# Start of the projections: small loads on ScalarE's queue, free signals first, first rows scaled at once, query weights a head per round

## The reference

```python
h = rms_norm(x, g_mix)
q, k, v, f_logit, a, gate = split(h @ w_in)        # 3 x 512, 8, 2 x 512 columns
logf = log_sigmoid(f_logit + b_f)                  # per row and head
attn = softmax(q k^T / 8 + cumsum(logf) terms, causal) v
u = a * sigmoid(gate)
conv = silu(layer_norm(depthwise_conv31(u) + b_dw))
x = x + concat(attn, conv) @ w_out
x = x + peer_ffn(rms_norm(x, g_ffn))               # 8 heads, 16 of 16384 experts each, rows gathered
y = rms_norm(x, g_final)
```

## Time and profile before

| | us |
|---|---|
| median of 3 runs | 3392.09 |
| lowest and highest | 3391.64, 3394.30 |
| the profiled execution | 3393.65 |
| its span, first to last instruction | 3391.9 |
| busy: TensorE 73%, DVE 72%, POOL 42%, ACT 30% of the span | |
| mean granted TensorE clock | 0.869 of full speed |
| gathers of expert rows (1088), share of the 16 DMA engines' span | 83.0% |
| query-weight loads | 8 of 1024 KB |
| store of turned keys, per round | 260 KB |

### The profile page before, as it was taken

One profiled execution on the slowest core, in us unless ns is written; L12 is line 12 of the kernel. 1 busy time (PEld: TensorE's weight loads), 2 busy tenths in 40 slices (PEclk: granted clock), 3 DMA queues, 4 the chain that ended last, 5 costly groups with the idle time before them and its releaser, 6 DMA issues. The chain is left out here.

```text
span 3391.9 us, 42114 instructions
## 1 busy us (share of the span) xinstructions
PE 2480.5 (73%) x13551; PEld 1076.9 (32%) x13551; DVE 2438.2 (72%) x6866; ACT 1021.4 (30%) x2925; POOL 1427.7 (42%) x1266
## 2 busy tenths in 40 slices
PE   5999867766866687767777776687767766776665
PEld 2444542322322233323323332333333322222221
DVE  2888757777777777777777776777677767677885
ACT  2333323223232323332333233323233233222321
POOL 0233344444444434443444444444444444444443
PEclk8999889888888888888888888888888888888887
DMA  7111429999999999999999999999999999999997
GB/s 253 56 56 47 134 110 412 416 415 403 415 407 410 399 411 403 408 406 410 400 405 399 410 404 401 404 405 401 408 400 412 405 411 409 388 392 420 419 414 313
DMA packets 220330, 1220.19 MB, mean 360 GB/s; under 512 B 34138, under 2 KB 61474, under 8 KB 80869
## 3 DMA queue, kind: packets, MB, share of 16 engines
q0 software_dynamic: 156672, 1140.92, 83.0%
q1 hardware_dynamic: 63461, 76.83, 6.8%
HBM read 1199.12 MB, written 18.55 MB: 359 GB/s over the span
## 5 line engine op out<-in xcount | busy, mean ns | idle before, releaser
L1269 POOL DMA_INDIRECT uv_rows<-in_uv_emb,experts x1088 | 1263.9, 1162 | 1607.1 <-PE ps L1373 1406.4
L1373 PE MATMUL ps<-uv_rows,diag 64*64 64x512 f32 x8704 | 1325.7, 734 | 823.8 <-ACT diag L1637 823.0
L1850 DVE CUSTOM_DVE_ANT_0 uv_rows<-uv_rows,handed 128x1024 f32<-128x1024 f32 x1088 | 1331.1, 1224 | 656.1 <-DMA uv_rows<-in_uv_emb,experts 651.0
L1373 PEld LDWEIGHTS ps<-uv_rows,diag 64*64 64x64 f32 x8704 | 321.7, 153 | 1477.1 <-ACT diag L1637 1059.4
L1629 ACT ACTIVATE gelu_c<-dots 128x2 f32<-128x2 f32 x544 | 110.7, 204 | 1649.6 <-DVE dots L1850 1648.6
L1637 ACT ACTIVATE diag<-ident_twice,act_c 128x64 f32<-128x64 f32 x1088 | 319.2, 340 | 283.9 <-DVE act_c L1867 282.9
L1333 PE MATMUL ps<-w_pq_sb,xnT_c 128*128 128x256 f32 x1152 | 342.7, 428 | 0.7 <-ACT xnT_c L1596 0.7
L1333 PEld LDWEIGHTS ps<-w_pq_sb,xnT_c 128*128 128x128 f32 x1152 | 219.9, 207 | 250.7 <-issue 227.4
L567 PE MATMUL ps<-w_in_sb,w_out_sb 128*128 128x512 f32 (+1 forms) x656 | 242.7, 525 | 17.5 <-ACT w_out_sb L453 17.5
L625 DVE SCALAR_TENSOR_TENSOR handed<-w_out_sb,tapsT,handed 128x128 f32<-128x128 f32 x960 | 252.8, 346 | 0.0
L388 POOL TENSOR_TENSOR rstd_a<-ms_a,neg_half 128x1 f32<-128x1 f32 x9 | 81.1, 9015 | 207.8 <-ACT ms_a L434 207.8
(11 more groups left out here) (247 smaller groups left out, 2166.8 us busy)
## 6 DMA issues: line engine op xcount, KB each, us to landing
uv_rows<-in_uv_emb,experts POOLq DMA_INDIRECT x1088, 13.2
w_in_sb<-in_w_in SPq DMA_DIRECT2D x4, 2048.0 KB, 12.0
w_pq_sb<-in_w_pq SPq DMA_DIRECT2D x8, 1024.0 KB, 12.3
w_out_sb<-in_x_prompt SPq DMA_DIRECT2D x8, 512.0 KB, 4.0
handed<-in_x_prompt SPq DMA_DIRECT2D x8, 512.0 KB, 3.4
w_out_sb<-in_w_out SPq DMA_DIRECT2D x1, 4096.0 KB, 19.2
out<-handed SPq DMA_DIRECT2D x8, 512.0 KB, 8.1
keys_turned<-handed SPq DMA_DIRECT2D x10, 260.0 KB
```

Of the source, the lines that this page charges most:

```text
L1269: nc.gpsimd.indirect_dma_start(out=rows[:, m % RING, :], out_offset=None, in_=d.uv_emb[0], in_offset=bass.IndirectOffsetOnAxis(ap=experts[ ...
L1373: ins = pe.matmul(ps[dst, 2 * x + half, :], diag[src, (m + i) % DIAGS, :], rows[src, (m + i) % RING, cols], start=first, stop=last)
L1850: nc.vector.tensor_tensor_reduce(out=row, in0=row, in1=xn[:, block_of(n) % 2, :], scale=1.0, scalar=0.0, op0=ALU.mult, op1=ALU.add, accum_ ...
```

## The change

The nine small loads are issued by ACT, ahead of its first mean square, with the cached log-forgets before the cached keys. SP's five increments stand right behind the load of block 0's rows, and all weights of w_in are issued without a break. `normed(0)` follows `row_scale(0)` directly, ahead of the copies of the setup. The query weights are loaded one head at a time: head b in `round_of(b)` right after the rows of the next block, the eighth after the sample rows.

```diff
--- before.py
+++ after.py
@@ -276,10 +276,8 @@
         @block.sync
         def _(sp):
             sp.dma_start(x[:, :], d.x_prompt[0, 0:P, :]).then_inc(x_here, 16)
-            sp.dma_start(vecs[0:s.DCH, :], d.g_mix[0].rearrange("(c p) -> c p", p=P)).then_inc(small_here, 16)
-            for i, v in enumerate((d.b_dw, d.ln_g, d.ln_b)):
-                lo = s.DCH + i * s.CCH
-                sp.dma_start(vecs[lo:lo + s.CCH, :], v[0].rearrange("(c p) -> c p", p=P)).then_inc(small_here, 16)
+            for stored, by in ((k_stored, 16), (kT_stored, 16), (q_stored, 16), (v_stored, 32), (conv_stored, 16)):
+                sp.sem_inc(stored, by)
             w_rows = d.w_in[0].rearrange("(c p) n -> p c n", p=P)
 
             def load_weights(name):
@@ -290,14 +288,12 @@
                     to = lo - s.DA if lo > COLS["v"][0] else lo
                     sp.dma_start(w_in[:, :, to:to + width], w_rows[:, :, lo:lo + width]).then_inc(w_here[name], 16)
 
-            load_weights(ORDER[0])
-            sp.dma_start(taps[:, :], d.w_dw[0]).then_inc(small_here, 16)
-            sp.dma_start(state[:, :], d.state_conv[0, 0]).then_inc(small_here, 16)
-            sp.dma_start(bf[:, :], d.b_f[0].partition_broadcast(P)).then_inc(small_here, 16)
-            sp.dma_start(k_aug[:, :, 0:s.HD], d.cache_k[0, 0]).then_inc(past_here, 16)
-            sp.dma_start(logf_past[:, :], d.cache_logf[0, 0]).then_inc(past_here, 16)
-            for name in ORDER[1:]:
+            for name in ORDER:
                 load_weights(name)
+
+            def load_query_weights(h):
+                hs = slice(h * 2 * s.HALF, (h + 1) * 2 * s.HALF)
+                sp.dma_start(g.w_pq[:, :, hs], d.w_pq[0][:, hs].rearrange("(c p) n -> p c n", p=P)).then_inc(g.w_pq_here, 16)
 
             def store_keysT(kb):
                 sp.dma_start(d.kT[:, :, bass.ds(kb * P, P)].rearrange("h e t -> e h t"), c.keysT).then_inc(kT_stored, 16)
@@ -324,21 +320,18 @@
             def round_of(b):
                 sp.wait_ge(xn_ready, b + 1)
                 sp.dma_start(x[:, :], d.x_prompt[0, bass.ds((b + 1) * P, P), :]).then_inc(x_here, 16)
+                load_query_weights(b)
                 if b > 0:
                     store_conv(b - 1)
                 stores(b, b, k_rows[bass.ds(b * P, P)], v_rows[bass.ds(b * P, P), :], P)
 
-            for stored, by in ((k_stored, 16), (kT_stored, 16), (q_stored, 16), (v_stored, 32), (conv_stored, 16)):
-                sp.sem_inc(stored, by)
             sp.wait_ge(kT_ready, PAST)
             store_keysT(s.NB)
-            for h in range(s.PH):
-                hs = slice(h * 2 * s.HALF, (h + 1) * 2 * s.HALF)
-                sp.dma_start(g.w_pq[:, :, hs], d.w_pq[0][:, hs].rearrange("(c p) n -> p c n", p=P)).then_inc(g.w_pq_here, 16)
             for b in range(s.NB - 1):
                 round_of(b)
             sp.wait_ge(xn_ready, s.NB)
             sp.dma_start(x[0:s.TS, :], d.x_sample[0]).then_inc(x_here, 16)
+            load_query_weights(s.PH - 1)
             store_conv(s.NB - 2)
 
             first = c.first
@@ -491,16 +484,25 @@
                 act.wait_ge(v_stored, 32 * b + 32)
                 each(b, nc.scalar.copy, c.values, ps[:, V_, :]).then_inc(v_ready, 1)
 
+            act.dma_start(vecs[0:s.DCH, :], d.g_mix[0].rearrange("(c p) -> c p", p=P)).then_inc(small_here, 16)
+            for i, v in enumerate((d.b_dw, d.ln_g, d.ln_b)):
+                lo = s.DCH + i * s.CCH
+                act.dma_start(vecs[lo:lo + s.CCH, :], v[0].rearrange("(c p) -> c p", p=P)).then_inc(small_here, 16)
+            act.dma_start(taps[:, :], d.w_dw[0]).then_inc(small_here, 16)
+            act.dma_start(state[:, :], d.state_conv[0, 0]).then_inc(small_here, 16)
+            act.dma_start(bf[:, :], d.b_f[0].partition_broadcast(P)).then_inc(small_here, 16)
+            act.dma_start(logf_past[:, :], d.cache_logf[0, 0]).then_inc(past_here, 16)
+            act.dma_start(k_aug[:, :, 0:s.HD], d.cache_k[0, 0]).then_inc(past_here, 16)
             for free in (q_ready, k_ready, v_ready):
                 act.sem_inc(free, 1)
             row_scale(0)
+            normed(0)
             act.wait_ge(setup_psum, 3)
             nc.scalar.copy(c.tapsT[:, :, :], ps[:, Q_, 0:s.CCH * s.TAPS].rearrange("p (c j) -> p c j", c=s.CCH)).then_inc(setup_sb, 1)
             nc.scalar.copy(g.vecT[:, :], ps[:, K_, 0:NVEC]).then_inc(setup_sb, 1)
             nc.scalar.copy(stateT[:, :, :], ps[:, V_, 0:s.CCH * HALO].rearrange("p (c j) -> p c j", c=s.CCH)).then_inc(setup_sb, 1)
             act.wait_ge(cum_psum, 1)
             nc.scalar.copy(cum_past[:, :], ps[:, F_, s.H:2 * s.H]).then_inc(cum_ready, 1)
-            normed(0)
             keys_out(PAST)
             SETUP_LINKS, LINKS = chain.n, 2
             with act.Fori(0, s.NB) as b:
```

## The result

The changed kernel takes 3373.13 us (median of six runs, 3372.05 to 3374.06) against 3392.38 beside it: a ratio of 0.9942, 95% interval 0.9931 to 0.9952. It is faster by 19.25 us, as forecast in sign and within the range of 3360 to 3384, but 7.5 us short of the forecast 3365.6.

The account below looks back on a forecast made before the run. TensorE bounds the projection rounds, DMA gathers the rest; two early stalls were removable. Round 1 starting at 60.9 instead of 87.42 saves 26.5 us: 3367.1 from the profiled run, 3365.6 from the median; range 3360 to 3384, own 3362 to 3370.

Parts of the forecast that it names:

- A: Rival on the setup loads: small loads land no earlier than before, ACT's descriptors waiting out SP's backlog; 3368.6 us, chance 0.19.
- B: Rival on load issue: ACT's issues block as SP's did, until 23.54 us; 3383.8 us, chance 0.13.
- Query weights a head per round: SP's queue in round 0: block 1's rows, freed of eight loads ahead, land at 38.7 us; spread loads stay hidden.
- D: Rival on later rounds: each spread query-weight load delays its round by 2.9 us, giving back 20; 3386 us, chance 0.05.
- First rows scaled at once: ACT's setup: scaling moves under the wait for small loads; worth zero, first rows scaled at 10.3 us.
- Small loads on ACT's queue: Setup before round 0: bias lands at 10.6 us, cached keys at 12.0; matmul on cached forget values moves from 15.30 to 12.0.
- Free signals first: Setup: ACT's copy of the turned cached keys starts at about 18.5 us instead of 23.75, no longer awaiting SP; 5.2 us.
- The sum: Rounds 0 to 1: u turned at the later of 42.4 and 42.8 us, plus 18.1 to round 1; 26.5 us less.
- T0: Start of round 0's first projection matmul, 26.55 us in the kernel before; forecast 18.0.
- T1: Start of round 1's first projection matmul, 87.42 us in the kernel before; forecast 60.9.
- The term of 1.9 us: Round 0's gate, a, f and k: 24.42 us exceed the steady 22.5 by 1.9, put on TensorE's granted clock.
- C: Rival on the setup loads: ACT's queue starves until SP's is empty at 37.7 us; 3395.4 us, slower, chance 0.03.

## Why the prediction was right, and where it was not

The time was forecast as a gain of 26.5 us from four parts; 19.25 came, from one of them. The measured 3373.13 lies above the forecast's own range (3362 to 3370), and inside 3360 to 3384 only because that also made room for rivals A and B, whose course did not come either. That much of the hit is luck.

*Query weights a head per round*: right. SP issued block 1's rows at 27.50 instead of 52.87, and their square started at 38.79; worked out were 38.7.

```profile
27.50 1.71 SPq L322 DMA_DIRECT2D w_out_sb<-in_x_prompt  x1
```

The 20.3 us too long in round 0 became 2.0 (69.15 - 26.56 - 40.6). The spread loads cost the later rounds nothing (pitch 40.58, from 69.15 to 109.73), so D is out.

*First rows scaled at once*: right, zero, in time (10.3) and in worth.

*Small loads on ACT's queue*: this step failed, and with it the size of the forecast. Its term was "I take these: the bias, issued at 3.4, lands at 10.6 ... the cached keys, issued at 4.5, land at 12.0". Measured: 14.38 and 20.47, later than my late bound (14.2 and 15.3). I had taken 7.2 us from a row in which a small load meets large gathers, but that load has 128 rows. By the packet counts above the cost of sharing goes by the rows a transfer has, not by its bytes, and the cached keys are 1024 rows. The bound "when they landed before" was no bound either: a second queue can be slower than its old place in the first. Rival A had the seven loads right (14.2) and the keys wrong.

*Free signals first*: the 5.2 us are right as a wait removed (ACT's row no longer names SP), but the keys' landing took the place of that wait to within 0.1 us. What the prediction called a sum was a maximum.

*The sum*: T0 26.56 for 18.0, u 51.06 for 42.8, T1 69.15 for 60.9. These 8.25 us are the whole miss at T1; the time missed by 7.5. The term of 1.9 us that the prediction put on TensorE's clock stands (last section).

Missing altogether was a rival: with T0 at 18.0 and u bound by block 1's rows at 42.8, the log-forgets come due as the convolution starts. That course was run (17.00 and 43.07), and in eight runs of ten it was no faster than the kernel before (3395.97 to 3399.16, against 3388.2 to 3397.9 beside it). Had the small loads landed as forecast, this kernel could have met that hold; that they landed late kept it clear, which is luck too. The sign to look for was in the profile: GpSimd's power, 0.56 us in the earlier trace rows, lasts 10 to 12 us in the later rounds, until the convolution ends, where it costs nothing.

B and C did not come: ACT's issues were over at 5.5, and TensorE started at 14.38, not after 37.

## What to carry to other kernels

Ask of each load who is behind it in its queue and when that one is wanted: eight early loads for a stage that was over 400 us away held up one block of rows for 25 us, and moving them was the whole gain. A second DMA queue does not give small rows a lane of their own; if they are wanted first, issue them first on the queue that carries the bulk. And when an edit makes a chain earlier, look what it will now run beside: an instruction on GpSimd that had finished ahead of a long DVE series may come to stand behind it.

## What the runs showed of the hardware that was not expected

- Two hardware queues share the DMA engines packet for packet (971 to 957 in 6 us), however unequal the packets: 2 KB and 256 bytes. A turn took 0.10 us beside rows of 2 KB and 0.02 beside rows of 32 bytes. 256 KB of cached keys took 15.6 us so, and 7.5 in the queue of the bulk.
- A GpSimd instruction of 0.25 us was held for 30.68 us beside a series of DVE instructions of 0.35 us each, until the series ended; in four other profiles the same instruction passed inside the same series in 0.41 or 0.42.
- The slow start of round 0's matmuls goes with TensorE's granted clock, as the prediction had it. In the kernel before, the clock is granted at 0.5 (1.2 GHz) from 23.30, in TensorE's idle 6.40 us, to 30.13 us, and at 1.00 (2.4 GHz) from then to 54.02, and the weight loads, one to a matmul, come 0.85 us apart before that moment and 0.43 after it. In the changed kernel they change their pace at 30.82 (weight loads of TensorE):

```profile
29.29 0.33 PEld L569 LDWEIGHTS ps<-w_in_sb,w_out_sb 128*128 128x128 f32 x1 [0.52 <-issue]
30.14 0.33 PEld L569 LDWEIGHTS ps<-w_in_sb,w_out_sb 128*128 128x128 f32 x1 [0.52 <-issue]
30.82 0.19 PEld L569 LDWEIGHTS ps<-w_in_sb,w_out_sb 128*128 128x128 f32 x1 [0.34 <-issue]
31.25 0.19 PEld L569 LDWEIGHTS ps<-w_in_sb,w_out_sb 128*128 128x128 f32 x1 [0.24 <-issue]
```
